# Causal pooling means on TensorE, from banded matrices over token-major tiles, in place of shift-and-add rows

## The chip, the cores and the metric

The kernel runs on one core of one Trainium2 chip. The metric is the device time of one execution in microseconds (us). The kernel does one inference step of a small two-layer decoder: layer 0 is a pooling mixer with a ConvFFN, layer 1 is dilated attention with a ConvFFN. Only the start of the program, the pooling mixer, is touched.

## The reference, cut to what matters

There are 1024 prompt tokens and 8 sample rows, and 1024 channels. The channels are four groups of 256, with windows of 2, 4, 8 and 16 tokens. Each token's normed row is replaced by (mean over its window) minus (itself), then mixed by a 256x256 matrix per group, scaled and added to the residual stream. A sample row takes its window from 15 stored rows and itself.

```python
def rms_norm(x, g):
    y = xf * lax.rsqrt(jnp.mean(xf * xf, axis=-1, keepdims=True) + NORM_EPS)
    return (y * g.astype(jnp.float32)).astype(x.dtype)

def pool_mixer(ext, n_hist, pos, w_pool, scale):
    ...
    for g, w in enumerate(POOL_WINDOWS):
        sl = slice(g * POOL_GROUP_W, (g + 1) * POOL_GROUP_W)
        lo = jnp.take(csum[..., sl], jnp.maximum(t_end - w, 0), axis=1)
        cnt = jnp.minimum(pos + 1, w).astype(jnp.float32)[None, :, None]
        parts.append((hi[..., sl] - lo) / cnt - cur[..., sl])
    d = jnp.stack(parts, axis=2)
    mixed = jnp.einsum('btgc,gce->btge', d, w_pool.astype(jnp.float32)).reshape(B, T, D)
    return (mixed * scale.astype(jnp.float32)).astype(ext.dtype)
...
    x = x + pool_mixer(ext, n_hist, pos, w_pool[layer], pool_scale[layer])
    new_pool.append(ext[:, -POOL_HIST:])
```

## The kernel before, in words

The residual stream `x` stands channel-major in SBUF: 8 chunks (`KC`) of 128 channels on the partitions, with N = 1032 columns (1024 tokens and 8 samples). The input arrives token-major in `xin`, 8 tiles of 128 tokens x 1024 channels, and `pe_start` turns it with 64 transposes; `dve_start` and `act_start` copy the turned groups out of PSUM (`pro_copy`, even groups on DVE, odd ones on ACT), while ACT also squares each token tile with a row sum. All order is written by hand: each engine has one program, and semaphores tie them together. Nothing is scheduled by a planner.

Matrix products of full fp32 accuracy are made in two ways. Most operands are split into a high part (`wh`, `xh`, rounded by ACT) and a low rest (`wl`, `xl`, a subtraction on DVE), and `group` (L324) multiplies them in three fast products, each as 3 matmuls of 344 columns. A few small products use plain fp32 matmuls, each of which the profile shows as two matmul instructions.

The pooling stage, in order:

- DVE computes the reciprocal root (`newton`, with ACT's Sqrt), spreads it into diagonal blocks `acc` (L507), PE sums them with `ones` into a broadcast row (L430), DVE copies it to `rb`, and 8 operations (L520) write the normed rows `xn`.
- `dve_windows` adds a shifted copy of a row to itself 1, 2, 3 or 4 times (L561 on DVE for even chunks, L583 on GpSimd for odd ones). `difference` divides, subtracts the row itself and patches the first 16 tokens and the samples (L537 to L546, five operations per chunk); ACT rounds to `xh` (L616), and `tail` writes `xl` (L552). The loop runs over four groups of two chunks, and a group's first row is added up only when the group before it has its `xl`.
- `pe_pool` mixes: per group two output chunks, 18 matmuls each (L324). DVE adds the result to `x` (L568), ACT squares and rounds it (L336, L340), DVE writes the low part (`dve_split`, L349), and GpSimd adds up the squares (L359).

Then comes the first ConvFFN. PE multiplies the first slab of `w_up` (72 matmuls of L324), then sums the squares with `ones` (L745); DVE and ACT make the reciprocal root of 1032 columns from it (L833 to L841), and from there PE works on slabs without a long pause.

## Time and profile before

| | |
|---|---|
| median of 3 runs | 2528.43 us (2525.35 to 2534.44) |
| span of the profiled execution | 2527.2 us |
| PE matmuls busy | 2345.1 us (93%) |
| DVE busy | 1408.1 us (56%) |
| ACT, GpSimd busy | 653.1 us (26%), 280.9 us (11%) |
| chain that ended last | PE 67%, issue 14%, DVE 7%, GpSimd 6% |

The profile is one execution. A line of groups gives what an engine did, on what tiles, how often and how long; the idle time before it has the releaser's name. The mean duration of an instruction is longer than the distance from one start to the next, because instructions overlap; where a stage is filled by a run of them, the distance counts. "PEclk" is the granted TensorE clock as a share of 2.4 GHz; it has two levels, 1.00 and 0.50 (1.2 GHz).

### The profile page before, as it was taken

The numbers are of one execution on the slowest core, as the hardware profiler recorded it, in microseconds if no ns is written. First come the engines' busy times: TensorE is split into PE (matmuls) and PEld (weight loads), VectorE is DVE, ScalarE is ACT, GpSimd is POOL, SyncE is SP. The second block draws the span as 40 slices with busy tenths as digits, with TensorE's granted clock in tenths as the row PEclk, the third lists the DMA queues.
The fourth block names the chain that finished last, engine by engine and source line by source line (L and its number), as shares of the span: only waits on it lengthen the run. The fifth ranks groups of instructions, "written<-read, shape, count | busy, mean of one in ns | idle before, by whom it ended". The sixth has DMA issues, their size and how long they took to land.

```text
span 2527.2 us, 40511 instructions
## 1 busy us (share of the span) xinstructions
PE 2345.1 (93%) x16139; PEld 2271.2 (90%) x16139; DVE 1408.1 (56%) x2057; ACT 653.1 (26%) x1120; POOL 280.9 (11%) x341
## 2 busy tenths in 40 slices
PE   4399999999999779999999798888999999999997
PEld 4399999999999769999999587578999999999996
DVE  6975555555555455462643577465655555555554
ACT  4332222222222232231221353222222222222222
POOL 1500000000000033241423220022000000000000
PEclk7699999999999889999999899989999999999999
DMA  5011111111111102222221686530111111111102
GB/s 156 0 51 50 46 46 50 41 50 33 50 50 50 47 24 93 74 79 93 79 86 39 185 291 205 154 123 26 51 50 50 46 45 50 41 50 41 50 25 71
DMA packets 164654, 179.41 MB, mean 71 GB/s; under 512 B 8207, under 2 KB 126751, under 8 KB 164290
## 3 DMA queue, kind: packets, MB, share of 16 engines
q1 hardware_dynamic: 164114, 177.58, 22.5%
q8 instruction: 68, 1.11, 0.2%
q10 hardware_dynamic: 440, 0.45, 0.1%
q14 instruction: 32, 0.26, 0.0%
HBM read 147.72 MB, written 38.01 MB: 73 GB/s over the span
## 4 chain that ended last, share of the span: by engine, by line
PE 67%; issue 14%; DVE 7%; POOL 6%; DMA 3%; ACT 1%; SPq 1%; POOLq 0%; DVEq 0%; ACTq 0%
PE ps L324 60%; POOL kn L1133 3%; PE ps L1385 2%; PE ps L1358 1%; POOL sq L1135 1%; POOL kn L1141 1%; PE ps L1369 1%; DMA kvt<-kvs 1%; PE ps L1327 1%; DVE swin L561 1%; PE ps L1397 1%; POOL sq L1138 1%; POOL sq L1136 1%; DVE xl L347 1%; PE ps L1350 1%
## 5 line engine op out<-in xcount | busy, mean ns | idle before, releaser
L324 PE MATMUL ps<-xh,wh 128*128 128x344 f32 x2160 | 462.6, 323 | 63.7 <-DVE x L568 39.2
L324 PE MATMUL ps<-xl,wh 128*128 128x344 f32 x2160 | 461.3, 322 | 0.0
L324 PE MATMUL ps<-xh,wl 128*128 128x344 f32 x2160 | 458.4, 321 | 0.0
L324 PEld LDWEIGHTS ps<-xh,wh 128*128 128x128 f32 x2160 | 366.2, 190 | 67.0 <-issue 56.5
L324 PEld LDWEIGHTS ps<-xl,wh 128*128 128x128 f32 x2160 | 368.3, 190 | 0.0
L324 PEld LDWEIGHTS ps<-xh,wl 128*128 128x128 f32 x2160 | 362.3, 189 | 0.0
L704 ACT ACTIVATE wh<-stage 128x1024 fp32r<-128x1024 f32 x132 | 137.3, 1058 | 762.4 <-PE ps L324 755.8
L821 DVE TENSOR_TENSOR x<-x,ps 128x1032 f32<-128x1032 f32 x176 | 216.2, 1229 | 124.2 <-PE ps L324 124.2
L785 DVE TENSOR_TENSOR ub<-ps,rb 128x1032 f32<-128x1032 f32 x44 | 54.2, 1233 | 374.6 <-PE ps L324 374.6
L324 PE MATMUL ps<-gh,wh 128*128 128x344 f32 x1056 | 227.7, 324 | 23.9 <-issue 16.1
L324 PE MATMUL ps<-gl,wh 128*128 128x344 f32 x1056 | 226.9, 323 | 0.0
L324 PE MATMUL ps<-gh,wl 128*128 128x344 f32 x1056 | 225.7, 322 | 0.0
L324 PEld LDWEIGHTS ps<-gh,wh 128*128 128x128 f32 x1056 | 180.2, 191 | 26.1 <-issue 21.2
L324 PEld LDWEIGHTS ps<-gl,wh 128*128 128x128 f32 x1056 | 179.0, 190 | 0.0
L324 PEld LDWEIGHTS ps<-gh,wl 128*128 128x128 f32 x1056 | 178.6, 190 | 0.0
L709 DVE TENSOR_TENSOR wl<-stage,wh 128x1024 fp32r<-128x1024 f32 x132 | 158.5, 1216 | 0.0
L359 POOL TENSOR_TENSOR acc<-acc,sq 128x1032 f32<-128x1032 f32 x21 | 53.1, 2529 | 836.2 <-ACT sq L336 835.8
L1161 PE MATMUL ps<-wp0h,xh 128*128 128x256 f32 (+1 forms) x432 | 121.9, 282 | 10.2 <-DVE xl L347 7.4
L785 DVE TENSOR_TENSOR ua<-ps,rb 128x1032 f32<-128x1032 f32 x44 | 54.2, 1233 | 134.6 <-PE ps L324 134.3
L1161 PE MATMUL ps<-wp1h,xh 128*128 128x256 f32 (+1 forms) x432 | 122.5, 283 | 0.6 <-DVE wp1l L1037 0.6
L1163 PE MATMUL ps<-wp1h,xl 128*128 128x256 f32 (+1 forms) x432 | 122.4, 283 | 0.0
L1162 PE MATMUL ps<-wp1l,xh 128*128 128x256 f32 (+1 forms) x432 | 121.9, 282 | 0.0
(244 smaller groups left out, 3797.8 us busy)
## 6 DMA issues: line engine op xcount, KB each, us to landing
stage<-in_w_up SPq DMA_DIRECT2D x88, 512.0 KB, 3.7
stage<-in_w_down SPq DMA_DIRECT2D x44, 512.0 KB, 3.6
stage<-in_w_kv SPq DMA_DIRECT2D x24, 512.0 KB, 4.3
kvs<-kn SPq DMA_DIRECT2D x48, 256.0 KB, 2.0
kvt<-kvs SPq DMA_DIRECT2D x16, 512.0 KB, 4.8
out_kv_w_prompt<-kvs SPq DMA_DIRECT2D x13, 512.0 KB, 6.6
om<-os_ SPq DMA_DIRECT2D x8, 792.0 KB, 5.7
...
```

The costliest lines, as they stand in the source:

```text
L324: mm = pe.matmul(ps[:, bank0 + c, 0:NW], w, m[:, c * NW:(c + 1) * NW], start=(i == 0), stop=(i == len(parts) - 1))
L347: nc.vector.tensor_tensor(xl[:, d, :], x[:, d, :], xh[:, d, :].bitcast(F32), ALU.subtract).then_inc(split_lo, 1)
L359: nc.gpsimd.tensor_tensor(acc[:, :], acc[:, :], sq[:, d % 2, 0:N], ALU.add).then_inc(split_acc, 1)
L704: nc.scalar.activation(wh[:, slot_of(k), :], stage[:, slot_of(k), :], ACT.Copy).then_inc(S.hi, 1)
L709: nc.vector.tensor_tensor(wl[:, slot_of(k), :], stage[:, slot_of(k), :], wh[:, slot_of(k), :].bitcast(F32), ALU.subtract).then_inc(S.lo, 1)
L785: nc.vector.tensor_tensor(cols3(u[:, 2:2 + N]), bank3(sset), cols3(rb[:, :]), ALU.mult).then_inc(free, 1)
L821: nc.vector.tensor_tensor(cols3(x[:, d, :]), cols3(x[:, d, :]), bank3(d % 2), ALU.add).then_inc(S.A if d % 2 == 0 else S.B, 1)
L1133: nc.gpsimd.tensor_tensor(row, row, per_head(hg[0:M, 1 if u else 0, :], HD), ALU.mult).then_inc(pj_r, 1)
L1161: pe.matmul(out, xh[:, k, tok], W[:, k, :], start=(k == 0), stop=False)
L1162: pe.matmul(out, xh[:, k, tok], Wt[:, k, :], start=False, stop=False)
L1163: mm = pe.matmul(out, xl[:, k, tok], W[:, k, :], start=False, stop=(k == KC - 1))
L1385: mm = pe.matmul(ps[:, 6, j * P:(j + 1) * P], probT[:, i % 2, n * P:(n + 1) * P], v, start=(w == 0), stop=(w == len(tiles) - 1))
```

## The change

The means are made by PE. For each chunk of 128 channels, every token tile of `xin`, scaled in place by its reciprocal root (token-major, so one number per partition), is the stationary operand, and a constant band matrix of up to 143 columns is the moving one: column j holds 1/count on the rows of j's window and an extra -1 on the row j itself. The up to 15 columns past the tile's edge fall into the next tile's outputs and add up there in PSUM. So `windows(c)` makes (mean minus itself) turned to channel-major, in 9 plain fp32 matmuls per chunk, 18 instructions. The gain g is put in where ACT and DVE read PSUM (`high`, `low`).

Gone are: `xn`, the broadcast of the reciprocal root (9 DVE operations, 3 matmuls of fp32, a copy), the window rows on DVE and GpSimd, and the five `difference` operations per chunk. New are 9 scalings on DVE (8 of 128x1024, one of 8x1024), 64 + 8 band matmuls, 16 small matmuls for the samples, and 4 small operations behind them. The root is taken in two parts, after token tile 3 and after the samples. The rows for the output buffers come from two GpSimd products with a broadcast copy of `g_pool`. `chin` is loaded earlier, and 590 KB of `band` and a 512 KB broadcast of `g_pool` are loaded besides. `mix(c - 2)` stands between `windows(c)` and `windows(c + 1)` on PE, all but the last mix in PSUM banks 0 to 2.

```diff
-            for c in range(KC):
-                nc.vector.scalar_tensor_tensor(out=xn[:, c, PAD:], in0=x[:, c, :], scalar=gT[:, G_POOL + c:G_POOL + c + 1],
-                                               in1=rb[:, :], op0=ALU.mult, op1=ALU.mult).then_inc(xn_v, 1)
...
+            def scaled(t):
+                v.wait_ge(pro_pe, 2 * t + 2)
+                nc.vector.tensor_scalar(xin[:, t, :], xin[:, t, :], rtok[:, t:t + 1], None, ALU.mult).then_inc(scl, 1)
...
+            for g in range(0, 12, 2):
+                turned(g)
+            stats(0, 4, 0, 1)
+            for t in range(2):
+                scaled(t)
+            turned(12)
+            scaled(2)
+            turned(14)
+            scaled(3)
+            stats(4, 9, 5, 2)
+            for t in range(4, 8):
+                scaled(t)
...
+            turned(16)
+            turned(19)
...
+            def low(c):
+                v.wait_ge(bd, c + 1)
+                v.wait_ge(dif_h, c + 1)
+                b = band_bank(c)
+                nc.vector.scalar_tensor_tensor(
+                    out=xl[:, c, 0:T].rearrange("p (b n) -> p b n", b=2), in0=ps[:, b:b + 2, :],
+                    scalar=gT[:, G_POOL + c:G_POOL + c + 1],
+                    in1=xh[:, c, 0:T].bitcast(F32).rearrange("p (b n) -> p b n", b=2), op0=ALU.mult,
+                    op1=ALU.subtract).then_inc(dif_l, 1)
...
+            low(0)
+            low(1)
+            samples()
+            for c in range(2, KC):
+                low(c)
+                add(c - 2)
+                if c == 3:
+                    dve_ffn_slab0(v, ffn[0])
+                if c > 3:
+                    dve_split(v, split[0], c - 4, G_FFN)
+            for d in range(6, KC):
+                add(d)
+                dve_split(v, split[0], d - 2, G_FFN)
+            for d in range(6, KC):
+                dve_split(v, split[0], d, G_FFN)
...
+            g.wait_ge(in_gb, 16)
+            g.wait_ge(scl, 9)
+            g.wait_ge(ssq, 9)
+            nc.gpsimd.tensor_tensor(rb[:, 0:D], xin[:, 7, :], acc[:, 0:D], ALU.mult).then_inc(tl_p, 1)
+            nc.gpsimd.tensor_tensor(sq[0:NS, 1, 0:D], xsin[:, :], acc[0:NS, 0:D], ALU.mult).then_inc(tl_p, 1)
...
+            def high(c):
+                act.wait_ge(bd, c + 1)
+                b = band_bank(c)
+                nc.scalar.activation(xh[:, c, 0:T].rearrange("p (b n) -> p b n", b=2), ps[:, b:b + 2, :], ACT.Copy,
+                                     scale=gT[:, G_POOL + c:G_POOL + c + 1]).then_inc(dif_h, 1)
...
+            for c in range(5, KC):
+                split_x(c - 5)
+                high(c)
+            for d in range(3, KC):
+                split_x(d)
...
+                if c == 0:
+                    pe.wait_ge(pro_a, 9)
+                    pe.wait_ge(pro_v, 10)
+                if c == 1:
+                    pe.wait_ge(pro_a, 10)
+                if c >= 2:
+                    pe.wait_ge(dif_h, c - 1)
+                    pe.wait_ge(dif_l, c - 1)
+                for t in range(8):
+                    if c == 0:
+                        pe.wait_ge(scl, t + 1)
+                    tok, k = xin[:, t, c * P:(c + 1) * P], 1 if t else 0
+                    at = t % 4 * P
+                    width = P if t in (3, 7) else P + halo
+                    mm = pe.matmul(ps[:, b + t // 4, at:at + width], tok, band[:, k, w, 0:width], start=(t == 0),
+                                   stop=(t in (3, 7)), skip_group_check=True)
...
+            pe.wait_ge(in_ph, 16 * 4)
+            windows(0)
+            windows(1)
+            samples()
+            for c in range(2, KC):
+                windows(c)
+                mix(c - 2)
+            mix(6)
+            mix(7)
```

On PE, before, the stretch from the broadcast of the root to the first mix reads so (the bracket is what an instruction waits for; `xn` are the normed rows, `dif_l` counts finished low parts):

```order
L430 MATMUL ps<-acc,ones 128x344 [waits dg,pro_a,set0,pro_v]
L430 MATMUL ps<-acc,ones 128x344 x2
L438 MATMUL ps<-ident,chin 128x32 [waits in_ch]
...
L438 MATMUL ps<-ident,chin 128x32 [waits rb_v,pro_a]
L438 MATMUL ps<-ident,chin 128x32 x11
L629 MATMUL ps<-ident,xn 23x128 [waits rb_v,xn_v]
L629 MATMUL ps<-ident,xn 23x128 x7
L324 MATMUL ps<-xh,wh 128x344 [waits pro_a,dif_l,pro_v,wp_l]
```

The same place in the changed kernel, from the last transposes to the first mix (`scl` counts scaled token tiles, `pro_v` and `pro_a` the copies of DVE and ACT, `ds_l` the samples' low part):

```order
L424 MATMUL ps<-ident,chin 128x32 x11
L628 MATMUL ps<-band,xin 128x129 [waits pro_v,scl,pro_a,in_ph]
L628 MATMUL ps<-band,xin 128x129 [waits scl] x2
...
L628 MATMUL ps<-band,xin 128x129 [waits pro_a]
...
L640 MATMUL ps<-sdiag,xsin 128x8 [waits pro_a,scl]
L640 MATMUL ps<-sdiag,xsin 128x8 x7
L643 MATMUL ps<-sel,phist 128x8 x8
L628 MATMUL ps<-band,xin 128x131 [waits dif_l,dif_h]
...
L320 MATMUL ps<-xh,wh 128x344 [waits vec,ds_l,pro_v,wp_l,dif_l]
```

The broadcast of the root and the transposes of `xn` are gone; two chunks of means and the samples stand ahead of the first mix, and the very first band matmul also waits for a count of DVE's copies.

On DVE, before, one group of two chunks (window 4) reads so, from its first addition to its low parts:

```order
L561 TENSOR_TENSOR swin<-xn 128x1039 [waits dif_h,dif_l]
L561 TENSOR_TENSOR swin<-swin 128x1037 [waits win_v]
L537 TENSOR_TENSOR swin<-swin,invc 128x16 [waits win_v]
L538 TENSOR_TENSOR swin<-hsum,xn 128x8
L539 SCALAR_TENSOR_TENSOR swin<-swin,xn 128x1008
...
L537 TENSOR_TENSOR sq<-sq,invc 128x16 [waits win_p]
L538 TENSOR_TENSOR sq<-hsum,xn 128x8
L539 SCALAR_TENSOR_TENSOR sq<-sq,xn 128x1008
...
L552 TENSOR_TENSOR xl<-swin,xh 128x1032 [waits dif_h]
L552 TENSOR_TENSOR xl<-sq,xh 128x1032 [waits dif_h]
```

In the changed kernel DVE's steady part of the stage reads so (L498 is `low`, L519 is `add`, L345 is `dve_split`; `bd` counts finished chunks of means, `pool_pe` finished mixes):

```order
L498 SCALAR_TENSOR_TENSOR xl<-ps,gT,xh 128x1024 [waits dif_h,bd]
L519 SCALAR_TENSOR_TENSOR x<-ps,gT,x 128x1032 [waits pool_pe]
L345 SCALAR_TENSOR_TENSOR xl<-x,gT,xh 128x1032 [waits split_hi]
L498 SCALAR_TENSOR_TENSOR xl<-ps,gT,xh 128x1024 [waits dif_h,bd]
L519 SCALAR_TENSOR_TENSOR x<-ps,gT,x 128x1032 [waits pool_pe]
L345 SCALAR_TENSOR_TENSOR xl<-x,gT,xh 128x1032 [waits split_hi]
```

Three operations per chunk are left there, each waiting for another engine, and the additions to `x`, which stood behind all four groups, stand between the low parts.

## Rows read from the trace of the kernel before

**Rows 1.** The page's first part: busy time, share of the span, instructions.

```profile
PE 2345.1 (93%) x16139; PEld 2271.2 (90%) x16139; DVE 1408.1 (56%) x2057; ACT 653.1 (26%) x1120; POOL 280.9 (11%) x341
```

**Rows 2.** Stretches: start:end length, busy per engine (instructions), PEclk, DMA share, GB/s.

```profile
34.00:52.00 18.00, 2.06 (x10) 1.15 (x9) 17.97 (x22) 3.79 (x5) 1.92 (x1) 0.50 0.33 93
61.00:94.00 33.00, 0.00 (x0) 0.00 (x0) 32.69 (x33) 5.26 (x5) 20.28 (x7) 0.56 0.00 0
94.00:122.50 28.50, 20.48 (x109) 19.75 (x109) 24.72 (x15) 12.46 (x13) 13.83 (x5) 0.85 0.00 1
```

**Rows 3.** The chain that ended last, in order of time: start, length, what.

```profile
84.28 2.83 DVE swin L561
...
122.46 13.11 PE ps L324 x72
135.57 1.75 PE ps L745 x6
```

**Rows 4.** Timeline of ACT at the start: start, length, engine, line, operation, tiles.

```profile
14.92 0.60 ACT L594 ACTIVATE x<-ps 128x512 f32<-128x512 f32 x1
...
20.90 0.18 ACT L597 ACTIVATION_READ_ACCUMULATOR sq<-xsin 8x1 f32 x1
21.10 1.28 ACT L599 ACT_TABLE_LOAD   x1
```

**Rows 5.** Timeline of DVE at the start.

```profile
13.39 0.69 DVE L496 COPY x<-ps 128x512 f32<-128x512 f32 x1 [0.18 <-PE ps L406]
...
22.64 0.21 DVE L459 RECIPROCAL rtok<-rtok 128x9 f32<-128x9 f32 x1 [1.35 <-ACT rtok L599]
...
23.50 1.66 DVE L507 TENSOR_SCALAR acc<-ident,rtok 128x128 f32<-128x128 f32 x8
25.07 0.23 DVE L509 TENSOR_SCALAR acc<-ident,rtok 128x8 f32<-128x8 f32 x1
```

**Rows 6.** Two lines' own views: duration in ns, shortest, median and longest.

```profile
L507 DVE TENSOR_SCALAR acc<-ident,rtok x8: 280/280/286, 23.5 to 24.9; 128x128 f32<-128x128 f32 x8
```

```profile
L1095 DVE TENSOR_SCALAR kn<-ps,rtok x27: 729/749/753, 985.1 to 1338.2; 128x512 f32<-128x512 f32 x24, 8x512 f32<-8x512 f32 x3
```

**Rows 7.** Timeline: three runs of plain fp32 matmuls on PE.

```profile
18.07 1.92 PE L420 MATMUL ps<-sel,phist 120*128 120x8 f32 x16 [0.31 <-DMA phist<-in_state_pool]
...
25.55 3.78 PE L430 MATMUL ps<-acc,ones 128*128 128x344 f32 x6 [5.56 <-DVE hsum L512]
```

```profile
1501.27 1.95 PE L1385 MATMUL ps<-kvt,probT 128*128 128x128 f32 x16
```

**Rows 8.** Timeline: first and last of the 12 triples of one group's mixes.

```profile
104.03 0.71 PE L324 MATMUL ps<-xh,wh 128*128 128x344 f32 x3 [0.81 <-DVE x L568]
...
109.30 0.64 PE L324 MATMUL ps<-xh,wl 128*128 128x344 f32 x3
```

**Rows 9.** Stretches with dense PE work; columns as in rows 2.

```profile
25.50:34.00 8.50, 8.45 (x50) 6.59 (x50) 4.60 (x4) 1.61 (x3) 0.00 (x0) 0.50 0.26 90
52.30:57.60 5.30, 5.29 (x18) 5.30 (x19) 5.23 (x3) 0.00 (x0) 5.22 (x2) 0.50 0.00 2
57.60:61.00 3.40, 3.21 (x19) 2.92 (x18) 3.40 (x11) 1.12 (x2) 0.48 (x1) 0.94 0.00 0
...
122.40:126.40 4.00, 3.94 (x15) 3.97 (x16) 3.02 (x2) 4.00 (x4) 2.72 (x2) 0.57 0.00 0
1501.20:1503.00 1.80, 1.80 (x19) 1.80 (x17) 1.25 (x3) 1.51 (x8) 0.00 (x0) 1.00 0.79 216
```

**Rows 10.** Lines' own views: durations of DVE operations of 1032 columns, as in rows 6.

```profile
L568 DVE SCALAR_TENSOR_TENSOR x<-ps,gT,x x8: 1276/1279/1287, 94.4 to 122.3; 128x1032 f32<-128x1032 f32 x8
```

```profile
L349 DVE SCALAR_TENSOR_TENSOR xl<-x,gT,xh x16: 1285/1877/3453, 98.0 to 1733.6; 128x1032 fp32r<-128x1032 f32 x16
```

```profile
L821 DVE TENSOR_TENSOR x<-x,ps x176: 1215/1229/1231, 200.2 to 2512.0; 128x1032 f32<-128x1032 f32 x176
```

**Rows 11.** A stretch of the loads; columns as in rows 2.

```profile
18.00:24.00 6.00, 1.92 (x16) 1.86 (x16) 1.40 (x8) 5.43 (x13) 0.00 (x0) 0.71 1.14 222
```

More of the change, by code:

```diff
@@ new lines, in pe_start @@
+            pe.wait_ge(pro_a, 5)
+            pe.wait_ge(in_v, 16 * 7)
+            pe.transpose(ps[:, 1, 0:48], vC[:, :], ident[0:48, 0:48])
+            pe.transpose(ps[:, 1, 48:136], vB[:, :], ident[0:88, 0:88])
+            for i in range(3):
+                mm = pe.transpose(ps[:, 1, 136 + 88 * i:224 + 88 * i], vA[:, i, :], ident[0:88, 0:88])
+            mm.then_inc(pro_pe, 1)
+            pe.wait_ge(in_ch, 16)
+            for q in range(3):
+                pe.wait_ge(*((pro_v, 7) if q == 1 else (pro_a, 6 + q // 2)))
+                for i in range(CH * q, min(CH * (q + 1), 2 * NF)):
+                    c = i - CH * q
+                    mm = pe.transpose(ps[:, 3 + q, 32 * c:32 * c + 32], chin[:, i * P:(i + 1) * P], ident[0:32, 0:32])
@@ L588, in act_start, with turned @@
+            def turned(g, s):
+                act.wait_ge(pro_pe, g + 1)
+                for dst, src in pro_copy(g):
+                    nc.scalar.activation(dst, src, ACT.Copy).then_inc(s, 1)
+            act.wait_ge(set0, 2)
             for t in range(8):
@@ L591, in act_start @@
                 nc.scalar.activation(sq[:, 0, 0:D], xin[:, t, :], ACT.Square, accum_out=rtmp[:, 3, t:t + 1]).then_inc(ssq, 1)
-                act.wait_ge(pro_pe, 2 * t + 2)
-                for dst, src in pro_copy(2 * t + 1):
-                    nc.scalar.activation(dst, src, ACT.Copy).then_inc(pro_a, 1)
+                turned(2 * t + 1, pro_a)
+                if t == 4:
+                    root(0, 4, 1)
             act.wait_ge(in_xs, 16)
```

322 lines of the change are left out of this document (123 added, 199 removed).

## The prediction

> **What bounds the kernel now.** I read four views. The page's first part has PE busy for 93% of the span [rows 1], so over the whole program PE's work is the bound, and only a stretch in which PE waits can give time back. The table of stretches shows where it waits: from 34 to 52 us PE works 2.06 of 18 us, from 61 to 94 us not at all, from 94 to 122.5 us it works 20.48 of 28.5 us; DVE is busy for 17.97, 32.69 and 24.72 us of them [rows 2]. The pooling stage is thus DVE's. The chain of waits says the same: it runs through DVE's shifted additions (2.83 us for one row of 1025 columns, beside GpSimd's) and then joins PE for good at 122.46 us, with the 72 matmuls of the first w_up slab (13.11 us) and the sum of squares, whose first matmul the timeline has at 135.4 us [rows 3]. Behind it the reciprocal root and the slabs are the same code in both kernels. So the whole sum is one number: **when does the slab's last matmul end**, now 135.4 us.
>
> **What goes.** The eight L520 operations, the 20 window rows, the 40 difference operations and L552 are the chain from about 30 to 94.5 us; none of them was hidden, since PE stood still [rows 2]. What is late next is the start of the band matmuls, then PE's own work.
>
> **The first part: when the band matmuls start.** Nothing changes until DVE's sixth copy (13.39 us + 0.69 [rows 5]). The first half of the root needs ACT: its copy for token tile 4 ends at 15.5 us, then comes the table load, 1.28 us, and a root of 0.2 us [rows 4], so 17.0. DVE's four Newton steps take 0.86 us (22.64 to 23.50 [rows 5]): 17.9. Two scalings, a copy, a scaling, a copy, a scaling follow. The copies are 0.66 us apart. **A scaling of 1024 columns isn't in the trace**; two readings bound it. L507 with 128 columns takes 280 ns, L509 with 8 takes 0.23 us [rows 5, 6]: 0.45 ns per column, or 226 + 1016 x 0.45 = 0.68 us. L1095, which reads PSUM, takes 749 ns for 512 [rows 6], 1.04 ns per column: 1.28 us. I take the first, since L507 also goes from SBUF to SBUF, and 0.62 us from start to start, as L507's starts are 0.07 us closer than its duration (8 in 1.66 us). So 17.9 + 4 x 0.62 + 2 x 0.66 = 21.7. The second half waits for ACT: the samples' square sum, now at 21.08, is later by the table load and the root, 22.6 [rows 4]. Scale, root and Newton, 0.17 + 0.2 + 0.86 and 0.1 for waits, give 24.0. Five more scalings: 27.1. Then PE waits not for the scalings but for `pro_v` at 10, DVE's copies 16 and 19 behind them, 0.9 us: **the first band matmul starts at 28.1**. At 1.28 us a scaling it would be 32.
> (The Trainium skill, "VectorE: DVE Perf Modes", section "The perf-mode tier table", gives fp32 `tensor_scalar` in SBUF a 2x mode that `tensor_tensor` and PSUM operands lack. By it the scaling is the 0.68 us of L507's slope; without it the sum would be 4 us longer.)
> The loads must not be later. 720 KB of `chin` and 590 KB of `band` now stand ahead of `phist`, for which PE waited until 18.07 us [rows 7]; at the 222 GB/s of 18 to 24 us [rows 11] that is 5.9 us, 24 us, so 4 us are free. At twice that, 30, it would cost 2. `w_pool` comes behind them too. Between it and the first mix, at 40 us, lie a rounding on ACT and a subtraction on DVE of 2048 columns, about 2.4 us each (twice L821's 1.23 [rows 10]), so it may land as late as 35. `tl_p` and the output rows are waited for by ACT only at some 50 us.
>
> **The second part: PE's work.** A chunk of means is 18 instructions (16 of 128 to 143 columns, 2 tiny). At the full clock L1385, the same form with 128 columns, has 16 in 1.95 us less the last one's overhang, 0.117 us each [rows 7]; with the wider ones and the tiny two 2.1 to 2.25 us per chunk, I take **2.2**. At half the clock L430 has 344 columns in 0.573 us [rows 7], 1.67 ns per column: 0.215 us, **3.65 us** per chunk. The samples' 32 instructions go by L420, 16 in 1.86 us of starts [rows 7]: **3.7 us** at either clock, as that time is the weights'. A mix is 18 matmuls: 36 in 5.75 us [rows 8], **2.85 us**; at half clock 18 in 5.3 [rows 9].
> Which clock? At 28 us PE has only turned tiles and has been at 0.50 since about 20.5 (0.71 as the mean of 18 to 24 us [rows 11]). Dense work from 52.3 brought it to 1.00 at about 57.8, from 122.46 at about 126.3 [rows 9]. So windows(0) runs at 1.2 GHz (3.65), windows(1) half and half (2.8), the samples 3.7: 38.3. Behind the thin samples I expect a fall in half of the cases, 3 us each; 1.5 us in the sum. Then six times windows and mix, 6 x (2.2 + 2.85) = 30.3: 70.1. mix(6) waits for add(5), as both use bank 0: 1.25 us [rows 10]. mix(6) and mix(7) 5.7: 77.0. The slab's 72 matmuls at full clock are 72 x 0.158 = 11.4: **88.4 us**. Its low parts are ready: DVE's last split ends at about 85, the eighth of the slab that needs it begins at 87.
>
> **What DVE does meanwhile.** Per chunk `low`, `add` and `split`. The first two read PSUM and one SBUF row: 1.22 us from start to start, as L568 is 1279 ns and, over the whole program, none of 176 L821 is above 1231 [rows 10]; so GpSimd doesn't hold them up. The split reads two SBUF rows: 1.3 us alone, up to 3.45 beside GpSimd [rows 10]. Together 3.7 to 5.4 us against PE's 5.05, and GpSimd has one addition per chunk, so seldom the upper end. ACT has three operations of 1.1 us. Hence PE sets the pace.
>
> **The sum.** 135.4 - 88.4 = 47.0 us earlier. 2528.4 - 47.0 = **2481 us**. The profiled span is 2527.2, about 1 us under the median of 2528.43; the shift is taken off the median. At the start of the slab a clock of 0.57 cost about 1.7 us before [rows 9], which is contained.
>
> **The rivals.**
> 1. *The clock stays at 0.50 through the stage.* For it: from 25.5 to 34 us PE was busy for 8.45 of 8.50 us, fp32 products and transposes, at 0.50; against it: fp32 products at 1.00 at 1501 us, and each dense run of mixes came up [rows 9]. Price: 1.45 us for each of six chunks of means and 0.85 for the second, 5.3 - 2.85 for each of 8 mixes, 1.7 at the slab, less the 1.5 already counted: 29 us, 2510. Chance 0.07.
> 2. *DVE becomes the bound*, the splits alternating with GpSimd: 5.4 for 5.05 us in four steps and 2 to 4 us of low parts that the slab waits for: 2484 to 2487. For it the 1877 ns median of L349 [rows 10]. Chance 0.15.
> 3. *The start is late*: loads at half the rate, or scalings at 1.28 us: +2 to +6, 2483 to 2487. Chance 0.13.
> 4. *Slower than before*: the band matmuls' weight loads do not hide. There are 144 instructions, each with new weights. The 47 us are gone when one takes 47 / 144 = 0.33 us more than 0.117, so from 0.44 us on; at 0.26 (the mean weight load of 2271.2 / 16139 = 0.14 us [rows 1] and 0.117 one behind the other) 2502 would come out, at 0.5 us 2536. Against it: L1385 has the same pairs at 0.117 [rows 7]. Chance 0.02.
> 5. *It doesn't do what it says*: something behind the slab was due anyway, say the second slab's weights. Their load starts when `w_pool`'s low part is there, some 11 us earlier than now; I see nothing. Chance 0.02.
>
> **How the numbers follow.** My forecast has 0.61. Measured differences under 0.3% (7.6 us) can't be told from none. Range: the lower end takes a clock that rises in windows(0), samples in half the time and a low median, -8 us: 2473. The upper end takes in rivals 2 and 3 and two falls of the clock, +14: 2495. Outside are rivals 1, 4 and part of 5, and what I don't see, about 0.15. Faster by over 0.3%: all but rival 4 and half of rival 5, 0.97; same 0.01; slower 0.02.
>
> **What would show it.** First band matmul at 28 us (rival 3: 31 or more); 18 starts in 3.6 us for windows(0) and 2.2 from windows(2) on; PEclk 1.00 from about 40 us (rival 1: 0.50 in the table of stretches to 100 us); scalings of 0.7 us, not 1.3; PE idle before mix(6) only, 1.2 us, and after the stage up to 1 us; the first slab's last matmul at 88 us, and everything behind it 47 us earlier. Wrong would be PE idle <- DVE xl ahead of windows or of the slab's later eighths (rival 2), or a slab loop that got longer.

## The result and the profile after

The changed kernel takes 2487.23 us, median of 4 runs (2485.08 to 2494.45), against 2529.39 (2525.35 to 2534.44) for the kernel before, 4 runs on the same chip. The ratio is 0.9838, 95% interval 0.9818 to 0.9857: 42 us faster. Predicted were 2481 us and a range of 2473 to 2495. The profiled execution is the slowest of the four runs, 2494.45 us with a span of 2492.6, so stretches are compared by their position, and the total by the medians.

The first part of the page answers to [rows 1]. PE has 135 instructions more and 16 us more to do, and its share rose from 93 to 95%; DVE lost 50 us.

```profile
PE 2361.2 (95%) x16274; PEld 2290.2 (92%) x16285; DVE 1358.2 (54%) x2005; ACT 652.4 (26%) x1120; POOL 258.2 (10%) x332
```

The same stretch as in [rows 2], and the two that follow in the new stage (start:end, length, busy time per engine with instructions, PEclk, DMA share, GB/s). From 34 to 52 us PE worked 2.06 of 18 us before; now it works all of them, but at a mean clock of 0.80. DVE has 3.9 us free from 61 to 79 us; from 79 to 90.5 it is never idle, with its last splits, but PE works on all the same.

```profile
34.00:52.00 18.00, 18.00 (x113) 17.86 (x114) 7.00 (x8) 4.55 (x5) 2.19 (x1) 0.80 0.24 65
61.00:79.00 18.00, 16.52 (x115) 16.27 (x114) 14.10 (x11) 11.54 (x12) 12.20 (x5) 1.00 0.00 0
79.00:90.50 11.50, 11.50 (x75) 11.50 (x75) 11.50 (x7) 6.13 (x6) 6.32 (x3) 1.00 0.00 1
```

The timeline of PE at the start of the stage (start, length, engine, line, operation, tiles, count, idle time ahead and its releaser) is the main view. L628 and L631 are the chunks of means, L640 and L643 the samples' thin products, L320 the first mix.

```profile
28.06 2.06 PE L628 MATMUL ps<-band,xin 128*128 128x129 f32 x8 [3.05 <-DVE convh L473]
...
34.06 1.29 PE L628 MATMUL ps<-band,xin 128*128 128x129 f32 x8
35.28 1.95 PE L640 MATMUL ps<-sdiag,xsin 8*128 8x8 f32 x16
37.16 3.03 PE L643 MATMUL ps<-sel,phist 120*128 120x8 f32 x16
40.04 2.09 PE L628 MATMUL ps<-band,xin 128*128 128x131 f32 x8
...
43.94 1.03 PE L320 MATMUL ps<-xh,wh 128*128 128x344 f32 x3
...
47.18 1.05 PE L628 MATMUL ps<-band,xin 128*128 128x131 f32 x8
```

The stretches over it show the clock. It comes up in 34 to 36 us, is down again from 38 to 44, and up for good from 46 us on. The two stretches in the middle are the first and the second 16 instructions of the samples (L640, L643): the first at full clock throughout, the second mostly at half.

```profile
34.00:36.00 2.00, 2.00 (x16) 1.88 (x16) 1.18 (x1) 0.61 (x1) 2.00 (x1) 0.90 0.01 3
35.28:37.16 1.88, 1.88 (x18) 1.86 (x17) 0.54 (x1) 1.11 (x1) 0.92 (x1) 1.00 0.09 15
37.16:40.04 2.88, 2.88 (x18) 2.88 (x17) 0.74 (x1) 0.00 (x0) 0.00 (x0) 0.61 0.70 185
42.00:44.00 2.00, 2.00 (x12) 2.00 (x11) 0.00 (x0) 0.00 (x0) 0.00 (x0) 0.50 0.06 12
46.00:48.00 2.00, 2.00 (x17) 2.00 (x16) 1.45 (x2) 0.39 (x1) 0.00 (x0) 1.00 0.00 0
```

The chain that ended last (start, length, what) answers to [rows 3]. It stays on PE from 28.06 us on, apart from one addition of DVE in front of mix(6), where PE idles 1.48 us; the slab's last matmul ends at 90.5 us, where the kernel before had 135.4.

```profile
71.98 1.30 DVE x L519
73.42 17.23 PE ps L320 x108
90.65 1.75 PE ps L773 x6
```

### The profile page after: what moved, and what is told of

The parts are those of the page before. It is cut to its first block, busy times and chain, and to the rows that moved or that the text cites. A ratio compares the mean times of both kernels' runs of the same rounds, so it can differ in the third digit from the quotient of the medians.

```text
span 2492.6 us, 40747 instructions
## 1 busy us (share of the span) xinstructions
PE 2361.2 (95%) x16274; PEld 2290.2 (92%) x16285; DVE 1358.2 (54%) x2005; ACT 652.4 (26%) x1120; POOL 258.2 (10%) x332
## 3 DMA queue, kind: packets, MB, share of 16 engines
q1 hardware_dynamic: 164274, 178.66, 22.7%
## 4 chain that ended last, share of the span: by engine, by line
PE 70%; issue 14%; POOL 6%; DVE 4%; DMA 3%; ACT 1%; SPq 1%; POOLq 0%; DVEq 0%; ACTq 0%
PE ps L320 61%; POOL kn L1161 3%; PE ps L1413 2%; PE ps L1386 1%; PE ps L1397 1%; POOL sq L1163 1%; POOL kn L1169 1%; PE ps L1355 1%; PE ps L1425 1%; PE ps L628 1%; POOL sq L1164 1%; POOL sq L1166 1%; DMA kvt<-kvs 1%; DVE xl L343 1%; DVE rb L863 1%
## 5 line engine op out<-in xcount | busy, mean ns | idle before, releaser
L320 PE MATMUL ps<-xh,wh 128*128 128x344 f32 x2160 | 460.0, 321 | 13.9 <-DVE wl L737 7.1
L320 PE MATMUL ps<-xl,wh 128*128 128x344 f32 x2160 | 458.8, 321 | 0.0
L320 PE MATMUL ps<-xh,wl 128*128 128x344 f32 x2160 | 456.4, 320 | 0.0
L320 PEld LDWEIGHTS ps<-xh,wh 128*128 128x128 f32 x2160 | 363.7, 188 | 16.1 <-DVE wl L737 7.4
L320 PEld LDWEIGHTS ps<-xl,wh 128*128 128x128 f32 x2160 | 365.9, 189 | 0.0
L320 PEld LDWEIGHTS ps<-xh,wl 128*128 128x128 f32 x2160 | 360.3, 188 | 0.0
L320 PE MATMUL ps<-gh,wh 128*128 128x344 f32 x1056 | 227.1, 324 | 24.3 <-issue 16.1
L320 PE MATMUL ps<-gl,wh 128*128 128x344 f32 x1056 | 226.8, 323 | 0.0
L320 PE MATMUL ps<-gh,wl 128*128 128x344 f32 x1056 | 224.9, 321 | 0.0
L320 PEld LDWEIGHTS ps<-gh,wh 128*128 128x128 f32 x1056 | 179.4, 190 | 26.6 <-issue 21.1
L320 PEld LDWEIGHTS ps<-gl,wh 128*128 128x128 f32 x1056 | 178.9, 190 | 0.0
L320 PEld LDWEIGHTS ps<-gh,wl 128*128 128x128 f32 x1056 | 178.0, 189 | 0.0
L1191 PE MATMUL ps<-wp0h,xl 128*128 128x256 f32 (+1 forms) x432 | 123.0, 285 | 0.0
L1190 PE MATMUL ps<-wp0l,xh 128*128 128x256 f32 (+1 forms) x432 | 122.3, 283 | 0.0
```

The lines of the kernel that those rows point to most:

```text
L320: mm = pe.matmul(ps[:, bank0 + c, 0:NW], w, m[:, c * NW:(c + 1) * NW], start=(i == 0), stop=(i == len(parts) - 1))
L1190: pe.matmul(out, xh[:, k, tok], Wt[:, k, :], start=False, stop=False)
L1191: mm = pe.matmul(out, xl[:, k, tok], W[:, k, :], start=False, stop=(k == KC - 1))
```

## The experiments

b1 is the kernel before once more and c3 a variant of it; all others are variants of the changed kernel. Each ratio is taken against runs of the kernel before on the same chip; their medians are 2528.0 (the a's), 2529.8 (the b's), 2530.4 (the c's) and 2528.5 us (d1), so the medians of different letters are compared by their ratios. "Slab end" is the start of the sum-of-squares matmuls, as in the prediction; it is 90.5 us in the changed kernel.

| kernel | median us (runs) | ratio, 95% interval | slab end | behind it |
|---|---|---|---|---|
| before | 2529.39 (4) | | 135.4 | 2391.8 |
| after | 2487.23 (4) | 0.9838 (0.9818 to 0.9857) | 90.5 | 2402.1 |
| a1_after_again | 2487.78 (4) | 0.984 (0.9823 to 0.9856) | 90.5 | 2394.2 |
| a2_samples_first | 2490.28 (4) | 0.9848 (0.9832 to 0.9865) | 90.6 | 2397.4 |
| a3_windows_twice | 2509.12 (1) | | 107.6 | 2399.7 |
| a4_low_twice | 2491.55 (1) | | 92.6 | 2397.1 |
| b1_before_again | 2531.71 (1) | | 134.4 | 2395.5 |
| b2_early_start | 2485.63 (4) | 0.9832 (0.9811 to 0.9852) | 87.7 | 2395.1 |
| b3_samples_between | 2493.03 (4) | 0.985 (0.9832 to 0.9868) | 96.5 | 2403.0 |
| b4_both | 2491.47 (4) | 0.9842 (0.9824 to 0.9861) | 93.6 | 2399.1 |
| c1_history_early | 2486.81 (4) | 0.9827 (0.9804 to 0.9851) | 85.9 | 2401.0 |
| c2_dense_idle | 2491.21 (4) | 0.9844 (0.9823 to 0.9864) | 88.6 | 2398.7 |
| c3_before_dve_windows | 2524.43 (1) | | 129.6 | 2393.0 |
| d1_all_three | 2485.11 (5) | 0.9825 (0.9806 to 0.9844) | 87.2 | 2397.3 |

"Behind it" is the profiled span less the slab end. The slab ends were the same to 0.1 us in the two profiles of the changed kernel and 1.0 us apart in the two of the kernel before, while what is behind them moved by 8 us in the changed one. So a step of the stage is judged by the slab end, and the medians only say whether it survived. Every variant has one profile only.

### Once more, the changed kernel and the one before

> The changed kernel once more, for a second profile. In the first one the slab's last matmul ended 44.9 us earlier than before (90.5 for 135.4), but the span was only 34.6 us shorter; 6.5 us went between the first and the last attention matmul. Theory: that is scatter of the attention stage from one execution to the next, so this profile's slab end is again at 90.5 +- 0.5, but its attention stage (first to last matmul of L1413) has another length than 218 us, and the ratio to before is 0.982 to 0.985. Rival: the change itself costs the later stages 6 to 10 us (another placement in memory): the stage is again 218 us for the 213 of before, and the span again 2492.

> The kernel before once more, for a second profile. From the slab's last matmul to the end of the span it took 2391.8 us in its first profile; the changed kernel and its relatives took 2394 to 2402. Theory (scatter of the attention stage and of the last outputs): the same stretch is now somewhere between 2391 and 2400, and the first slab's end is at 135.4 +- 0.5. Rival (the change costs the later stages about 4 us): it is again within 1 us of 2391.8.

The second profile of the changed kernel has the same stage (90.5) and 7.9 us less behind it, with 213.8 us of attention instead of 218.2, as the theory said; its median is 2487.78. The first profile was thus a long one, not a sign that the stage's gain is lost. The second profile of the kernel before has 2395.5 behind the slab, inside the theory's range, and a slab end of 134.4, outside of its 135.4 +- 0.5. The section on why comes back to what these two have in common with the others.

### The mean's matmuls twice

Every chunk's loop of nine banded products is issued a second time into the same place.

```
+                for again in range(2):
                     for t in range(8):
                         ...
```

> Every band matmul is issued twice (the second round starts the sum anew, so the result is the same). Theory (PE sets the pace, one chunk of means costs 2.0 us at the full clock and 3.9 at the half): slab end later by 16 to 19 us, 107 to 110. Rival (DVE or ACT set the pace and PE has slack): under 12 us. Rival (weights of the band matmuls do not hide, dearer than 0.12 us each): over 25 us.

The slab end moved from 90.5 to 107.6, 17.1 us for 8 x 18 instructions: 2.14 us per chunk, 0.119 us each. The step "2.2 us per chunk, with weight loads that hide behind the matmuls" is measured by this. PE's wait in front of mix(6) is 1.48 us here too, so the added instructions found no slack to hide in: they are path.

### DVE's subtraction twice

From chunk 2 on, DVE does the low part (L498, 1.28 us) twice.

```
+                if c >= 2:
+                    nc.vector.scalar_tensor_tensor(out=xl[:, c, 0:T]..., ...).then_inc(more, 1)
+                    v.wait_ge(more, c - 1)
                 nc.vector.scalar_tensor_tensor(out=xl[:, c, 0:T]..., ...).then_inc(dif_l, 1)
```

> DVE does the low part (L498, 1.28 us) twice for chunks 2 to 7, the same operation on the same data. Theory (PE sets the pace; DVE has 3.8 to 4.1 us per chunk for PE's 4.95): slab end later by 0 to 2 us, 90.5 to 92.5. Rival (DVE is the bound, or its operations lie in the chain from a mix to the next): 6 x 1.2 = 7 us later, 97 to 98.

Six more operations of 1.28 us, 7.7 us of DVE work, cost 2.1 us (92.6), just past the theory's 92.5. The timeline of PE names 1.2 us of it: three short waits and the one in front of mix(6), 1.88 instead of 1.48 us.

```profile
49.82 0.71 PE L320 MATMUL ps<-xh,wh 128*128 128x344 f32 x3 [0.28 <-DVE x L526]
...
70.56 0.71 PE L320 MATMUL ps<-xh,wh 128*128 128x344 f32 x3 [0.24 <-DVE x L526]
75.52 0.72 PE L320 MATMUL ps<-xh,wh 128*128 128x344 f32 x3 [1.88 <-DVE x L526]
```

DVE isn't the bound, but its margin per chunk is under 1.3 us. That excludes rival 2 for the changed kernel and says how near it was.

### The samples in front of the means, and spread among them

First the 16 thin products (8 columns each, 32 instructions) stand in front of windows(0); then they are spread over windows(1), four instructions behind each token tile (`sample(t)` is the pair of products, from `xsin` and from `phist`, of chunk t).

```
             pe.wait_ge(in_ph, 16 * 4)
+            samples()
             windows(0)
             windows(1)
-            samples()
```

> The 16 small matmuls of the samples stand ahead of windows(0) on PE, so that nothing thin lies between the band matmuls and the mixes. Theory (the thin stretch is behind the fall of the clock to 0.50 at 38 us, and so behind windows(2) at 3.9 us and the slow start of mix(0)): samples at 27.1 for 6 us at the half clock, windows(0) 3.9, windows(1) 2.6, windows(2) 2.0, mix(0) 2.9, so mix(0) ends at about 44.5 instead of 47.2 and the slab at 87.8 instead of 90.5; PEclk stays 1.00 from windows(1) on. Rival (the clock falls for another reason, or comes up late whatever stands there): mix(0) ends at 47 or later, slab at 90.5 to 91.

The slab end stayed, at 90.6. PE's timeline of this kernel shows what was given and taken: the 32 thin instructions take 34.17 - 27.26 = 6.9 us instead of 4.8, windows(2) waits 0.54 and the mix 0.91 us.

```profile
27.26 3.55 PE L640 MATMUL ps<-sdiag,xsin 8*128 8x8 f32 x16 [2.56 <-issue]
30.73 3.58 PE L643 MATMUL ps<-sel,phist 120*128 120x8 f32 x16
34.17 2.07 PE L628 MATMUL ps<-band,xin 128*128 128x129 f32 x8
...
41.17 1.13 PE L628 MATMUL ps<-band,xin 128*128 128x131 f32 x8 [0.54 <-DVE xl L498]
...
44.33 0.71 PE L320 MATMUL ps<-xh,wh 128*128 128x344 f32 x3 [0.91 <-issue]
```

Its stretches have the clock at 0.50 under the thin ones, and once it is up behind them it doesn't fall:

```profile
27.26:34.17 6.91, 6.91 (x33) 6.88 (x33) 4.44 (x3) 1.91 (x1) 4.84 (x2) 0.50 0.46 172
...
36.00:38.00 2.00, 2.00 (x12) 2.00 (x11) 0.00 (x0) 0.00 (x0) 0.03 (x1) 0.50 0.29 48
38.00:40.00 2.00, 2.00 (x16) 2.00 (x16) 0.26 (x1) 1.11 (x1) 0.00 (x0) 0.81 0.84 233
40.00:44.00 4.00, 2.88 (x24) 2.52 (x22) 2.77 (x5) 1.51 (x3) 0.00 (x0) 1.00 0.52 145
```

So neither expectation came in whole: the clock did what the theory says, and the slab end is the rival's. What is measured cleanly is the price of one instruction of a thin plain fp32 matmul: 32 in 6.9 us, **0.216 us each at 0.50**, against 16 in 1.88 us, 0.117 us, at 1.00 (L640 in the changed kernel).

```
                 for t in range(8):
                     ...
+                    if c == 1:
+                        sample(t)
```

> The samples' 16 small matmuls are spread over windows(1), two behind each token tile, instead of standing in one block behind it. Theory (a block of thin matmuls lets the clock fall): PEclk stays 1.00 from about 33 us on, windows(1) with the samples ends at 38.5, mix(0), which now waits for low(1) as in a2_samples_first, at 44.5, slab end 88 (2.5 us earlier). Rival (the thin ones let it fall wherever they stand): windows(1) with the samples ends at 40.5 or later, slab end 90 or later.

The rival came in, and by more than it said: slab end 96.5 instead of 90.5. windows(1) with the samples lasts until 45.9 us, windows(2) until 49.8, and the clock, at 0.50 since windows(0), comes up only behind them:

```profile
36.00:40.00 4.00, 4.00 (x16) 3.39 (x15) 0.00 (x0) 0.00 (x0) 0.40 (x1) 0.50 0.45 108
40.00:44.00 4.00, 4.00 (x15) 3.47 (x16) 0.00 (x0) 0.00 (x0) 0.00 (x0) 0.50 0.64 178
44.00:48.00 4.00, 4.00 (x18) 3.75 (x19) 1.64 (x3) 1.15 (x2) 0.00 (x0) 0.50 0.00 0
48.00:52.00 4.00, 4.00 (x20) 4.00 (x21) 0.82 (x2) 2.04 (x3) 0.00 (x0) 0.65 0.01 4
```

PE is shown as busy for all of these 16 us. Between 32 and 45.9 us a stream that mixes wide and 8-column matmuls didn't bring the clock up here, while windows(0) and windows(1) without them brought it up at about 34 us.

### An earlier start, and both

DVE's copies 16 and 19, for which the first band matmul waits, go ahead of the last scalings, and the band gets a semaphore of its own.

```
             turned(14)
             scaled(3)
+            turned(16)
             stats(4, 9, 5, 2)
+            turned(19)
             for t in range(4, 8):
                 scaled(t)
...
-            pe.wait_ge(in_ph, 16 * 4)
+            pe.wait_ge(in_bd, 16)
             windows(0)
             windows(1)
+            pe.wait_ge(in_ph, 16 * 3)
             samples()
```

> DVE does its copies 16 and 19 ahead of the second half of the scalings, and the band has a semaphore of its own, so that windows(0) starts when the last transposes are done, each tile as it is scaled, and doesn't wait for the other loads. Theory (these waits cost PE 3 us and nothing else is due there): first band matmul at 25.0 to 25.5, windows(0) over at 29, everything behind it 3 us earlier: slab end 87.3 to 88. Rival A (the band lands only at about 28 us): first band matmul still at 27.5 or later. Rival B (w_pool's low part on DVE, beside GpSimd's two products until 34 us, is due next): windows(2) waits for DVE xl and the gain is under 1.5 us.

PE turns the conv states until 25.3 us and goes on with the band at once; no idle time is shown in front of it, and the slab end is 87.7, both as the theory said:

```profile
20.78 4.59 PE L424 MATMUL ps<-ident,chin 32*128 32x32 f32 x44
25.30 2.09 PE L627 MATMUL ps<-band,xin 128*128 128x129 f32 x8
```

2.76 us earlier at the start, 2.8 at the end: what the start gives arrives whole. The clock fell again in the samples (0.50 from 36 to 40 us). The edit moves two things, the copies and the band's semaphore, but the loads were not what PE had waited for: in c1_history_early below, with the same loads as the changed kernel, PE passes the wait for all four and begins the products of `phist` at 25.06 us.

> b2 and b3 in one. Theory: windows(0) over at 29, windows(1) with the samples at 35.5, then the chain high(1), low(1), mix(0) at 38.1, slab end 84.5, 6 us earlier than the changed kernel, and a median near 2482. Rival (DVE's low part of w_pool and low(0) behind it are due next): windows(2) waits for DVE until 35.5 or more, slab end 86.5 or later.

With the samples spread as well it is 93.6, far from the theory's 84.5: against b3_samples_between the start gives its 2.9 us, and the spreading costs its 6 in the same way. No wait for DVE is shown, so the rival's reason isn't it; for 20 us PE is busy all the time at half clock:

```profile
24.00:44.00 20.00, 20.00 (x84) 17.91 (x84) 9.84 (x9) 4.52 (x4) 6.71 (x2) 0.50 0.55 177
```

### The history early, and dense work in the wait

PE waits 3.05 us in front of windows(0). The first kernel puts the history's 8 thin products (16 instructions) there, which need nothing but loads; the second puts 6 dense 128x128 products of the identity there, whose result nobody reads.

```
             pe.wait_ge(in_ph, 16 * 4)
+            pe.wait_ge(pro_a, 8)
+            for c in range(KC):
+                pe.matmul(ps[:, 7, (KC + c) * NS:...], phist[:, c * P:(c + 1) * P], sel[:, c // 2, :], ...)
             windows(0)
...
             def samples():
...
-                for c in range(KC):
-                    mm = pe.matmul(ps[:, 7, (KC + c) * NS:...], phist[:, c * P:(c + 1) * P], sel[:, c // 2, :], ...)
```

> Of the 32 thin instructions of the samples, the 16 that need only the loaded history (phist times sel) move from behind windows(1) to in front of windows(0), where PE waits 2.4 to 3.1 us for DVE in the changed kernel. Theory (the thin ones are path time, 3.0 us of the 4.8 at half clock): they run from about 25 to 28.3 us, windows(0) starts at 28.1 to 28.6 instead of 28.1, the samples behind windows(1) last 1.9 instead of 4.8 us, the slab's last matmul ends at 87.5 to 88.3 instead of 90.5, median 2484 to 2486. If 1.9 us of thin ones no longer bring the clock down, windows(2) and mix(0) run at full clock and it ends at 85.5 to 86.5, 2482. Rival A (the history lands too late): windows(0) starts at 29 or later, slab end 89 or more. Rival B (thin ones in front keep the clock low longer): windows(1) lasts 3.7 instead of 3.3 and the end is 88.5 to 89.5.

The slab end is 85.9, the lowest of all, 4.6 us earlier; this is the theory's second branch (85.5 to 86.5). The median, 2486.81, isn't the 2482 that it named.

```profile
25.06 3.58 PE L664 MATMUL ps<-sel,phist 120*128 120x8 f32 x16
28.49 2.07 PE L628 MATMUL ps<-band,xin 128*128 128x129 f32 x8
...
35.69 1.95 PE L640 MATMUL ps<-sdiag,xsin 8*128 8x8 f32 x16
37.57 1.16 PE L628 MATMUL ps<-band,xin 128*128 128x131 f32 x8
...
39.60 0.72 PE L320 MATMUL ps<-xh,wh 128*128 128x344 f32 x3
```

The samples take 1.88 instead of 4.76 us (-2.9), the start is 0.43 later, and windows(2) takes 39.60 - 37.57 = 2.03 instead of 3.90 us and its mix 2.92 instead of 3.24 (-2.2), since the clock stays up:

```profile
38.00:40.00 2.00, 2.00 (x20) 2.00 (x19) 0.88 (x4) 0.38 (x2) 0.00 (x0) 1.00 0.68 192
```

So 2.4 us come from moving the work into the wait. The other 2.2 us hang on a clock that held in this one profile; whether it would hold in the next isn't shown, and in d1_all_three below it fell.

```
             pe.wait_ge(in_ph, 16 * 4)
+            pe.wait_ge(pro_a, 8)
+            for c in range(6):
+                pe.matmul(ps[:, 7, 0:P], ident[:, :], ident[:, :], start=True, stop=True)
             windows(0)
```

> Six additional 128x128 matmuls of the identity with itself (12 instructions, some 2.6 us at half clock), whose result nobody reads, stand in PE's wait in front of windows(0); the rest is the changed kernel. Theory (in that wait PE does nothing, and the clock comes up the later for it): windows(0) starts as before at 28.1 and the clock is at 1.00 two to three us earlier, so windows(0) takes 3.3 instead of 3.9 and windows(1) 2.1 to 2.6 instead of 3.3; the slab's last matmul ends at 88.5 to 89.7 instead of 90.5. Rival (the wait has no part in it, the clock rises as late as before): windows(0) and windows(1) 3.9 and 3.3 us, slab end 90.5. Median 2486 to 2488 in both, so the stretches tell them apart.

The clock came up 4 us earlier, more than the theory's two to three, and the slab end is 88.6, inside its range. It fell again within the 32 thin instructions (33.40 to 37.44 us):

```profile
28.00:30.00 2.00, 2.00 (x12) 2.00 (x12) 0.41 (x1) 1.56 (x1) 0.99 (x1) 0.53 0.30 118
30.00:32.00 2.00, 2.00 (x21) 2.00 (x20) 2.00 (x1) 0.44 (x1) 2.00 (x2) 1.00 0.44 159
...
36.00:38.00 2.00, 2.00 (x14) 2.00 (x14) 0.36 (x3) 0.00 (x0) 0.00 (x0) 0.68 0.41 79
```

So the idle time of PE in front of its stage isn't free here: PE pays for it with half the clock in the matmuls behind it. The median, 2491.21, didn't follow the 1.9 us.

### The kernel before without GpSimd's rows

DVE does the odd chunks' window rows as well, ten additions more; GpSimd has none.

```
                 dve_windows(v, 2 * g, swin, win_v, ...)
+                dve_windows(v, 2 * g + 1, sq, win_p, ...)
...
-            for i in range(4):
-                if i:
-                    g.wait_ge(dif_l, 2 * i)
-                dve_windows(g, 2 * i + 1, sq, win_p, ...)
```

> The kernel before with the window rows of the odd chunks (10 additions that GpSimd does) on DVE too; GpSimd does none. Theory (DVE and GpSimd take turns on rows in SBUF, so that GpSimd's help was worth little): DVE's six additions of 2.83 us fall to 1.24 (-9.5 us), ten more come at 1.24 (+12.4), so the slab's last matmul ends at 137 to 140 instead of 135.4 us, and no addition is above 1.3 us. Rival (DVE's additions between summed rows cost 2.8 us by themselves, whatever GpSimd does): the six stay at 2.83 and six of the new ones cost the same, so +22 us, 157.

Of the theory the half on the additions came in (none is above 1.3 us), but its sum had the wrong sign: the stage isn't 2 to 5 us longer but 5 to 6 us shorter, slab end 129.6 against 134.4 and 135.4. The rival was wrong in both. DVE's six additions of two rows in `swin` took 2.83 us each before; here, as its own line shows (ns, shortest, median, longest):

```profile
L561 DVE TENSOR_TENSOR swin<-swin x6: 1228/1236/1239, 53.3 to 78.8; 128x1037 f32<-128x1037 f32 x3, 128x1033 f32<-128x1033 f32 x2, 128x1025 f32<-128x1025 f32 x1
```

Ten additions more at 1.24 us and six at 1.24 instead of 2.83 make the +2.9 us of the theory. What it had missed is a small operation behind them: L537, 16 columns, 0.17 us by itself, stood for 1.77, 1.76 and 2.20 us in the three larger groups of the kernel before, while GpSimd finished its row:

```profile
87.13 2.20 DVE L537 TENSOR_TENSOR swin<-swin,invc 128x16 f32<-128x16 f32 x1
```

That is 5.2 us. The subtraction of 2048 columns ahead of the rows (L528) went from 3.62 to 2.28 us as well. Together these put the end of DVE's last low part 4.2 us earlier; the rest of the difference lies behind it and isn't explained. The Trainium skill, "SBUF — State Buffer", section "SBUF: two separate sides", states the general form, that a DVE operation with two SBUF inputs and a GpSimd operation that reads SBUF hold the shared port pair one after the other, for the whole instruction. The trace of the kernel before agrees: GpSimd's first addition, which began 0.44 us ahead of L528, took 1.92 us, and it was L528 that got longer; GpSimd's additions beside DVE's additions took 2.8 to 2.97 us.

### The three steps together

The history's loads go ahead of the conv states, its products behind the transposes of `xsin` in the prologue, and DVE's copies forward.

```
             sp.dma_start(xsin ...)
+            sp.dma_start(sel ...).then_inc(in_ph, 16)
+            sp.dma_start(phist ...).then_inc(in_ph, 16)
             sp.dma_start(chin ...)
...
+            pe.wait_ge(pro_v, 6)
+            pe.wait_ge(in_ph, 16 * 2)
+            for c in range(KC):
+                pe.matmul(ps[:, 2, (KC + c) * NS:...], phist[:, c * P:(c + 1) * P], sel[:, c // 2, :], ...)
             pe.wait_ge(in_v, 16 * 7)
...
+            turned(16)
             stats(4, 9, 5, 2)
-            for t in range(4, 8):
+            for t in range(4, 7):
                 scaled(t)
+            turned(19)
+            scaled(7)
```

> The changed kernel with three steps together: DVE's copies 16 and 19 ahead of the last scalings and the band on its own semaphore (as in the early start), and the history samples in PE's wait of the prologue, for which sel and phist are loaded ahead of chin; the history goes to bank 2. Theory: PE does the 16 history instructions between 18 and 21.4 us while it would wait for the vectors, the turned conv states end at about 27, the first band matmul is at 26.5 to 27.5 (after: 28.1), the samples behind windows(1) last 1.9 us and no fall of the clock follows, so the slab's last matmul ends at 83.5 to 85 instead of 90.5. The rest of the program stays between 2394 and 2403 us, so the median is 2478 to 2487, most likely 2481 to 2484. Rival A (the loads were the bound: chin and the vectors come 1.3 us later and everything behind them too): first band matmul at 28 or later, slab end 85.5 to 86.5, 2485. Rival B (what is saved in this stage comes back behind the slab): slab end as in the theory, the rest 2401 us or more and the median not under 2486.

Rival A came in by its start, with a slab end 0.7 us past its range. The history's products cost no time, at 18.23 us and at full clock, but its loads pushed the vectors from 19.7 to 22.7 us, and with them the conv states' transposes:

```profile
18.23 1.92 PE L414 MATMUL ps<-sel,phist 120*128 120x8 f32 x16
22.74 0.31 PE L419 MATMUL ps<-ident,vC 48*128 48x48 f32 x1 [2.59 <-DMA vA<-in_conv_w]
...
23.76 4.90 PE L430 MATMUL ps<-ident,chin 32*128 32x32 f32 x44
28.59 2.09 PE L634 MATMUL ps<-band,xin 128*128 128x129 f32 x8
```

The first band matmul is at 28.6, the slab end at 87.2. Behind its 16 thin instructions the clock fell, where it had not in c1_history_early at nearly the same time:

```profile
36.00:38.00 2.00, 2.00 (x16) 1.98 (x16) 1.33 (x2) 0.56 (x1) 0.28 (x1) 0.83 0.29 47
38.00:40.00 2.00, 2.00 (x11) 2.00 (x11) 0.53 (x3) 0.26 (x1) 0.00 (x0) 0.50 0.74 194
```

Its median of 2485.11 is the lowest of all, but its ratio, 0.9825 (0.9806 to 0.9844), can't be told from that of the changed kernel.

## Why the prediction was right, and where it was off

The forecast named one number, the slab end: 88.4 us. It is 90.5. By the prediction's own steps:

| step | predicted | measured |
|---|---|---|
| first band matmul | 28.1 | 28.06 |
| scaling of 1024 columns | 0.68, every 0.62 | 0.746, every 0.67 |
| windows(0), windows(1) | 3.65, 2.8 | 3.87, 3.35 |
| samples | 3.7 | 4.76 |
| fall of the clock behind them | 1.5 allowed | 1.85 + 0.35 |
| a further chunk with its mix | 5.05 | 4.95 |
| wait in front of mix(6) | 1.25 | 1.48 |
| mixes 6 and 7, slab | 5.7, 11.4 | 5.72, 11.35 |

**The start.** It came in to 0.1 us, by its own mechanism, though with two small errors that cancel: the second root was ready 0.3 us before the 24.0 of the sum, and the scalings behind it took 0.3 us more. The timeline names DVE's copy (`convh`) as what PE waited for, not a load and not a scaling. Rival 3 is out: the scaling's 0.746 us lies by L507's slope (0.68) and not by the PSUM row (1.28), and `w_pool` landed at 28.2, long before 35. b2_early_start shows that those copies were what stood in the way, and c1_history_early that the loads were not.

**The samples: the step that failed.** I wrote that they take 3.7 us "at either clock, as that time is the weights'", and took 16 in 1.86 us from L420 [rows 7]. They took 4.76 us. The row of L420 begins at 18.07 us; the stretch from 18 to 20 us in the kernel before has PEclk 1.00:

```profile
18.00:20.00 2.00, 1.92 (x16) 1.86 (x16) 0.00 (x0) 2.00 (x6) 0.00 (x0) 1.00 1.21 288
```

I had read the clock from the mean of 18 to 24 us (0.71, [rows 11]) and knew that it falls at 20.5, so the row was one at full clock. At half clock the same instruction takes 0.216 us (a2_samples_first), nearly twice. In the changed kernel the first 16 ran at 1.00 (35.28 to 37.16, 1.88 us) and the second 16 at a mean of 0.61 (2.88 us). The records of the weight loads themselves have medians of 187 ns at 1.00 (L640 in the changed kernel) and 328 ns at 0.50 (L640 in a2_samples_first). The Trainium skill, "TensorE: Matmul & The Clock Gate", section "LDWEIGHTS (loading the stationary operand)", gives a weight load a time from its column count alone, P / 1.2 ns for P columns; an estimate from it is 107 ns for 128. The row at 1.00 is near it (0.117 us), the one at 0.50 isn't (0.216 us); the measurement decides, and the weight load of a plain fp32 matmul does follow the clock here.

**The clock.** "Behind the thin samples I expect a fall in half of the cases, 3 us each" was right in kind: it fell in both profiles of the changed kernel, and cost 2.2 us against the 1.5 in the sum. The rise at the beginning of the stage came later than I took (0.50 until 34 us; windows(1) took 0.55 us more). The fall's 0.7 us over the sum, the late rise's 0.55, the samples' 1.1 and windows(0)'s 0.2 make 2.5 us; the steady part gave 0.6 back and the wait took 0.2, which leaves the 2.1 us by which the slab end is late. Rival 1, a clock that stays down, didn't occur in the changed kernel, but b3_samples_between is that rival on a small scale: some 22 us at 0.50, and 6 us of price.

**DVE and rival 2.** The splits (L345) have a median of 1.29 us, where L349 had 1.88 [rows 10], and 3.46 only at the longest; PE waited for DVE once behind the start, and the slab ran without a stall. a4_low_twice measures the margin. Rival 4 is excluded by a3_windows_twice at 0.119 us per instruction. Rival 5 named a slab loop that waits for its weights: from the slab end to the first conv state, the first run of slabs takes 722.5 or 722.6 us in all fourteen profiles, so it isn't that.

**Behind the slab.** The prediction took everything behind the slab as unchanged, only earlier. The slab end is 44.9 us earlier, the medians are 42.2 apart. All profiles can be laid side by side, by the same landmarks; the mean granted clock stands behind the stroke.

| profile | attention's mixing | the end, from the last conv state on | all behind the slab |
|---|---|---|---|
| before, b1, c3 | 212.9 / 0.98, 214.5 / 0.97, 210.9 / 0.98 | 25.8 / 0.97 in each | 2391.8, 2395.5, 2393.0 |
| after | 218.2 / 0.96 | 26.8 / 0.99 | 2402.1 |
| a1, b2 | 213.8 / 0.98, 213.7 / 0.98 | 27.8 / 0.94, 26.7 / 0.99 | 2394.2, 2395.1 |
| a2, a4 | 211.5 / 0.98, 214.1 / 0.98 | 30.1 / 0.74, 29.7 / 0.75 | 2397.4, 2397.1 |
| a3 | 214.2 / 0.98 | 28.8 / 0.92 | 2399.7 |
| b4 | 216.2 / 0.96 | 26.8 / 0.99 | 2399.1 |
| c2, d1 | 216.6 / 0.97, 217.1 / 0.97 | 27.7 / 0.94 in each | 2398.7, 2397.3 |
| b3, c1 | 220.0 / 0.96, 217.0 / 0.97 | 29.8 / 0.75, 29.9 / 0.75 | 2403.0, 2401.0 |

The packed stretches move less: besides the 722.5 or 722.6 us of the first run of slabs, the start of layer 1 with its projections takes 558.5 to 563.1, what lies between attention and the second sum of squares 119.2 to 122.1, and the second run of slabs, from there to its last conv state, 751.0 to 752.5. What moves more are two stretches in which PE is not packed: attention, 211 to 220 us, and the program's end. In the end's last part, where PE works in pieces between DVE's copies, the clock either holds or drops; before and in c1_history_early:

```profile
2515.40:2519.40 4.00, 2.13 (x16) 1.71 (x16) 1.50 (x3) 1.31 (x3) 0.00 (x0) 1.00 0.90 273
```

```profile
2475.00:2479.00 4.00, 2.93 (x13) 2.15 (x11) 0.85 (x2) 0.76 (x2) 0.00 (x0) 0.50 0.77 218
```

The three profiles with the old stage have a mean of 2393.4 behind the slab, the eleven with the new one 2398.6: 2.9 us of it in attention, 2.5 in the end. That is enough for the missing 2.7 us, and for more. It is hardly chance: the end takes 25.8 us in each of the three and at least 26.7 in each of the eleven, and in all nine rows of the first table with the new stage and four runs or more the median, against that of the kernel before on the same chip, fell by less than the slab end did, by 2.1 (b3) to 7.6 us (c2); for the changed kernel run again it is 40.2 against 44.9 us. But what in the new stage does it **stays open**: the code and the data behind the slab are the same, and no run moved the whole rest of the program by a chosen time, which would tell whether it is a matter of when these stretches begin. It fits, too, that the medians hardly rank the variants, though their slab ends are 85.9 to 96.5: c1_history_early gained 4.6 us in the stage and had 2401.0 behind it.

So the forecast held by its mechanism, and its error of 6 us has these parts: 2.1 us in the stage, of which half is a price read at the wrong clock, and 2.7 us behind it, which the sum had put at nothing; 1 us is that the sum was made from a median of 2528.4 and the four runs of the kernel before that stand beside the changed one have 2529.4, and the rest is rounding.

## What to carry to other kernels

When a price is taken from a row of TensorE, take the granted clock of that very stretch with it, also for matmuls that seem bound by their weights: plain fp32 ones with 8 columns cost 0.117 us per instruction at 1.00 and 0.216 at 0.50. Thin matmuls belong into a wait that is there anyway (2.4 us here, without the clock's part), and in one block, not spread through dense work (slab end 90.5 against 96.5); what keeps a dense stage from starting is worth moving even by 3 us, as the start's gain arrived whole. Judge such steps by a landmark in the trace that repeats to 0.1 or 1 us, when the total scatters by 8, take a second profile where the step hangs on the clock, and ask of work shared between DVE and GpSimd what DVE would take alone.
